# Rotary halves exchanged by on-chip transfers instead of a permutation product

## The reference

```python
def apply_rope(x, cos, sin):
    d2 = x.shape[-1] // 2
    x1, x2 = x[..., :d2], x[..., d2:]
    ...
    return jnp.concatenate([x1 * c - x2 * s, x1 * s + x2 * c], axis=-1)
```

## Time and profile before

| | |
|---|---|
| three runs | 1240.99, 1241.23 and 1244.12 us, median 1241.23 |
| the profiled execution | 1241.36 us, span 1239.5 us, 1.9 us around it |
| PE busy | 1217.6 us, 98% of the span |
| DVE, ACT, POOL busy | 848.9, 633.9 and 65.7 us |
| TensorE clock | 0.999 of full speed |

### The profile page before, as it was taken

How to read it: one execution, slowest core, us unless ns; L and a number is a source line. 1 busy time by engine, 2 the same in 40 slices (tenths; PEclk the granted TensorE clock), 3 DMA queues, 4 the chain that set the end, 5 groups by cost and what they waited for, 6 DMA issues and landing times. The chain is left out here.

```text
span 1239.5 us, 19652 instructions
## 1 busy us (share of the span) xinstructions
PE 1217.6 (98%) x7540; PEld 1064.9 (86%) x7540; DVE 848.9 (68%) x1241; ACT 633.9 (51%) x949; POOL 65.7 (5%) x58
## 2 busy tenths in 40 slices
PE   8999999999999999999999999999999999999997
PEld 6888889989998888888998888888899988888886
DVE  5776666667866766666799666666568976765564
ACT  6554456365536544445755555444475464544443
POOL 0000000300000000000430000000003200000000
PEclk9999999999999999999999999999999999999999
DMA  9575565565345665556555156555644724656550
GB/s 290 175 234 179 193 181 146 135 181 175 122 137 187 204 196 178 197 175 187 163 119 171 35 173 222 182 190 183 196 136 124 158 103 141 198 189 204 176 196 34
DMA packets 200914, 209.57 MB, mean 169 GB/s; under 512 B 58137, under 2 KB 177553, under 8 KB 200849
## 3 DMA queue, kind: packets, MB, share of 16 engines
q1 hardware_dynamic: 200400, 208.21, 54.2%
q10 hardware_dynamic: 448, 0.46, 0.1%
HBM read 207.61 MB, written 1.05 MB: 168 GB/s over the span
## 5 line engine op out<-in xcount | busy, mean ns | idle before, releaser
L1416 DVE TENSOR_TENSOR w_lo<-raw,w_hi 128x2048 fp32r<-128x2048 f32 (+2 forms) x192 | 433.0, 2257 | 174.0 <-ACT w_hi L1045 173.6
L2031 PE MATMUL bank<-n_both,w_hi 128*128 128x512 f32 x1216 | 432.8, 399 | 1.6 <-DVE w_lo L1416 1.6
L1045 ACT ACTIVATE w_hi<-raw 128x2048 fp32r<-128x2048 f32 (+2 forms) x192 | 360.7, 1880 | 97.9 <-PE bank L1970 76.2
L2032 PE MATMUL bank<-n_both,w_lo 128*128 128x256 f32 x1216 | 341.4, 281 | 0.0
L2031 PEld LDWEIGHTS bank<-n_both,w_hi 128*128 128x128 f32 x1216 | 228.5, 188 | 58.1 <-DVE w_lo L1416 1.5
L2032 PEld LDWEIGHTS bank<-n_both,w_lo 128*128 128x128 f32 x1216 | 229.7, 189 | 1.9
L1970 PE MATMUL bank<-n_both,w_hi 128*128 128x256 f32 (+3 forms) x960 | 175.9, 285 | 0.0
L1970 PE MATMUL bank<-w_hi,hid_hi 128*128 128x512 f32 x440 | 172.6, 392 | 0.2 <-DVE hid_lo L1497 0.2
L1970 PE MATMUL bank<-w_lo,hid_hi 128*128 128x512 f32 x440 | 171.7, 390 | 0.0
L1970 PE MATMUL bank<-w_hi,hid_lo 128*128 128x512 f32 x440 | 171.6, 390 | 0.0
L1063 ACT ACTIVATE scr<-bank 128x256 f32<-128x256 f32 x152 | 50.0, 381 | 207.5 <-PE bank L2032 207.5
(11 more groups left out here) (266 smaller groups left out, 1407.1 us busy)
## 6 DMA issues: line engine op xcount, KB each, us to landing
raw<-in_w_ff_dram SPq DMA_DIRECT2D x64, 1024.0 KB, 5.1
raw<-in_w_in_dram SPq DMA_DIRECT2D x31, 1024.0 KB, 5.3
raw<-in_ffn_down_dram SPq DMA_DIRECT2D x22, 1024.0 KB, 4.9
raw<-in_ffn_up_dram SPq DMA_DIRECT2D x21, 1024.0 KB, 5.3
raw<-in_ffn_gate_dram SPq DMA_DIRECT2D x20, 1024.0 KB, 5.3
raw<-in_w_out_dram SPq DMA_DIRECT2D x12, 1024.0 KB, 5.1
raw<-in_w_in_dram SPq DMA_DIRECT2D x12, 256.0 KB, 4.0
raw<-in_w_uq_dram SPq DMA_DIRECT2D x24, 128.0 KB, 3.9
```

Of the source, the lines that this page charges most:

```text
L1045: nc.scalar.activation(wh(s)[:, c0:n], raw[:, s % RING, c0:n], ACT.Copy).then_inc(hi_ready, 1)
L1416: V.tensor_tensor(wl(s)[:, c0:n], raw[:, s % RING, c0:n], wh(s)[:, c0:n].bitcast(f32), ALU.subtract).then_inc(lo_ready, 1)
L2031: MM(pb[:, :], w(s, 0)[:, c], n_both[:, k].rearrange("p a t -> p (a t)"), start=(k == 0), stop=False, skip_group_check=True)
L2032: return MM(pb[:, 0:T], w(s, 1)[:, c], xn(k, 0), start=False, stop=(k == KD - 1), skip_group_check=True)
```

## The change

PE's permutation product is gone, with its two matrices. In its place POOL issues transfers from SBUF to SBUF, one for each half, which bring the tile into a swap buffer with the halves exchanged: 4 transfers of 32 partitions where d2 is 32, and 8 of 16 partitions where it is 16. That is 28 in layer 0 and 48 in each of layers 1 and 2, 124 in all. POOL issues them in the rope step, ahead of its cosine product. The sign has moved into the sine tables. DVE waits for the landing, multiplies in place in the swap buffer, and adds as before. Layer 0 has two swap buffers and the others three, one of them `turn_s`.

Some steps stand elsewhere: sq1's rotation behind the first gate, ak's behind cq1's projection (and `toks` with it), kr's behind `uq` 0, uq's behind `ukv`; and DVE splits the second projection's slab behind the low halves, not ahead of them. The banks of the `wb` jobs are now given by number.

```diff
     rows = np.arange(P)
-    put("inv64", inv(32)[rows % 32][:, None])
+    put("inv64", sign(32) * inv(32)[rows % 32][:, None])
...
     put("cos_i", np.cos(angles(16, rows)))
-    put("sin_i", np.sin(angles(16, rows)))
+    put("sin_i", sign(16) * np.sin(angles(16, rows)))
 
     gamma = np.log1p(-np.exp2(-5.0 - np.arange(4)))
...
-    S += scores[0] + [("rope", 0, "nq1"), ("proj", 0, "sq1"), ("cmpt", "k")] + scores[1] + [("rope", 0, "sq1")] + turned[0]
-    S += gate[0] + [("cmp2", "k")] + scores[2] + weighted[0] + turned[1]
+    S += scores[0] + [("rope", 0, "nq1"), ("proj", 0, "sq1"), ("cmpt", "k")] + scores[1] + turned[0]
+    S += gate[0] + [("rope", 0, "sq1"), ("cmp2", "k")] + scores[2] + weighted[0] + turned[1]
...
-              ("stat", n), ("tables", l, "32"), ("tables", l, "64"), ("rope", l, "qi"), ("rope", l, "ak"),
-              ("toks", l), ("proj", l, "cq1"), ("rope", l, "ki"), ("proj", l, "cq2"), ("sums", l, 0),
+              ("stat", n), ("tables", l, "32"), ("tables", l, "64"), ("rope", l, "qi"),
+              ("proj", l, "cq1"), ("rope", l, "ak"), ("toks", l), ("rope", l, "ki"), ("proj", l, "cq2"), ("sums", l, 0),
...
-              ("rope", l, "rk"), ("proj", l, "rv"), ("rope", l, "rq"), ("rope", l, "kr"), ("rows", l),
-              ("uq", l, 0), ("ret", l, 0), ("ret", l, 1), ("ret", l, 2), ("ret", l, 3),
+              ("rope", l, "rk"), ("proj", l, "rv"), ("rope", l, "rq"), ("rows", l),
+              ("uq", l, 0), ("rope", l, "kr"), ("ret", l, 0), ("ret", l, 1), ("ret", l, 2), ("ret", l, 3),
               ("topk", l, 1, 0, 4), ("topk", l, 1, 4, 8), ("proj", l, "rg"), ("uq", l, 1),
-              ("retv", l), ("retn", l), ("rope", l, "uq"), ("uq", l, 2), ("s", l, "dsa", 0, 0),
-              ("s", l, "dsa", 0, 1), ("s", l, "dsa", 1, 0), ("s", l, "dsa", 1, 1), ("ukv", l),
+              ("retv", l), ("retn", l), ("uq", l, 2), ("s", l, "dsa", 0, 0),
...
+        swap = [swap0, wflat[:, 1536:2048], turn_s]
...
-                    job(("wb", 2 * n))
-                    job(("wb", 2 * n + 1), of_slab=True)
+                    job(("wb", 2 * n), 4 + 2 * n)
+                    job(("wb", 2 * n + 1), 5 + 2 * n, of_slab=True)
                 OT[st] = ohi[0]
...
+        SWAP, _landed, _user = {}, [0] * 3, [None] * 3
+        for u, r in RO.items():
+            b = r % 2 if u[0] == 0 else (r - RO[(u[0], "qi")]) % 3
+            _landed[b] += 16 * (8 if u[1] in ("qi", "ki", "kr", "uq") else 4)
+            SWAP[u] = (b, _landed[b], _user[b])
+            _user[b] = r
...
                     r = RO[st[1:]]
-                    src, n, nrow, _, (cos, _), dst = rotation(*st[1:])
+                    src, n, half, (cos, _), dst = rotation(*st[1:])
+                    b, _, user = SWAP[st[1:]]
+                    if user is not None:
+                        pool.wait_ge(rope_done, user + 1)
+                    if b == 2:
+                        pool.wait_ge(*((merged, 4) if st[1] == 1 else (oc_ready, NT + st[1] - 1)))
+                    pool.wait_ge(*free_count(XSC[st[1:]][0]))
+                    for c in range(0, P, half):
+                        other = c ^ half
+                        nc.gpsimd.dma_start(swap[b][c:c + half, 0:src.shape[1]], src[other:other + half]).then_inc(swap_in[b], 16)
                     pool.wait_ge(*free_count(XSC[st[1:]][0]))
                     pool.wait_ge(tab_ready, table_count(*st[1:]))
                     if r >= 2:
...
-                        ahead(SL[("proj", 0, "nq0") if n == 1 else ("proj", n // 2 - 1, "qi")], 1)
+                        first = SL[("proj", 0, "nq0") if n == 1 else ("proj", n // 2 - 1, "qi")]
+                        ahead(first, 0)
                         lower(n, (0, 1))
                         up_to_date(n, 3)
                         lower(n, range(2, 8))
+                        ahead(first, 1)
                     if n in (0, 2, 4, 5, 7):
                         take_mean(n).then_inc(mean_ready, 1)
...
                     r = RO[st[1:]]
-                    _, n, nrow, _, (_, sin), dst = rotation(*st[1:])
-                    pb = await_bank(dve, st)
+                    _, n, _, (_, sin), dst = rotation(*st[1:])
+                    b, landed, _ = SWAP[st[1:]]
+                    there = swap[b]
+                    dve.wait_ge(swap_in[b], landed)
                     dve.wait_ge(tab_ready, table_count(*st[1:]))
                     if st[2] == "kc":
-                        view = [x[:, 0:32].rearrange("p (g c) -> p g c", g=2)[:, :, 0:NCMP] for x in (turn_s, pb, turn_c[:, r % 2])]
+                        view = [x[:, 0:32].rearrange("p (g c) -> p g c", g=2)[:, :, 0:NCMP] for x in (there, turn_c[:, r % 2])]
                         s_ = sin[:, 31:T:16].unsqueeze(1).to_broadcast([P, 2, NCMP])
                     else:
-                        view = [x[0:nrow, 0:n * T].rearrange("p (a t) -> p a t", a=n) for x in (turn_s, pb, turn_c[:, r % 2])]
-                        s_ = sin.unsqueeze(1).to_broadcast([nrow, n, T])
-                    take_turn()
-                    V.tensor_tensor(view[0], view[1], s_, ALU.mult).then_inc(freed(st), 1)
-                    dve.wait_ge(*free_count(st))
+                        view = [x[:, 0:n * T].rearrange("p (a t) -> p a t", a=n) for x in (there, turn_c[:, r % 2])]
+                        s_ = sin.unsqueeze(1).to_broadcast([P, n, T])
+                    link(V.tensor_tensor(view[0], view[0], s_, ALU.mult))
                     dve.wait_ge(turnc_ready, r + 1)
                     if st[2] == "kc":
                         for g in range(2):
                             c = slice(64 * g, 64 * g + 64)
-                            last = V.tensor_tensor(kcR[c, g, 0:NCMP], view[2][c, g], view[0][c, g], ALU.add)
+                            last = V.tensor_tensor(kcR[c, g, 0:NCMP], view[1][c, g], view[0][c, g], ALU.add)
                         last.then_inc(rope_done, 1)
                     else:
-                        V.tensor_tensor(dst, view[2], view[0], ALU.add).then_inc(rope_done, 1)
-                    turn_used[0] = (rope_done, r + 1)
+                        V.tensor_tensor(dst, view[1], view[0], ALU.add).then_inc(rope_done, 1)
+                        if b == 2:
+                            turn_used[0] = (rope_done, r + 1)
                 elif kind == "xpe":
                     v = "kv".index(st[1])
                     if v == 0:
...
                         mm.then_inc(filled(("ukv", st[1], 2 + t)), 1)
-                elif kind == "rope":
-                    src, n, nrow, perm, _, _ = rotation(*st[1:])
-                    pe.wait_ge(*free_count(XSC[st[1:]][0]))
-                    pb = take(pe, st)
-                    if st[2] == "kc":
-                        mm = MM(pb[:, 0:32], perm, xs1[:, 0, 0:32], start=True, stop=True)
-                    else:
-                        mm = MM(pb[0:nrow, 0:n * T], perm, src, start=True, stop=True)
-                    mm.then_inc(filled(st), 1)
```

More of the change, by code:

```diff
@@ L50 @@
 NGAIN = _at
[L53 removed]
+CONST1 = [("ident", 128), ("inv64", 1), ("blk", 8), ("fold", 32),
           ("causal", 256), ("cmp_vis", 256), ("cos_a", 256), ("sin_a", 256), ("band", 256), ("cmp_mask", 256)]
@@ L77, in put, with sign @@
         where[:value.shape[0], at:at + n] = value
[L79 to L84, removed]
-            else:
-                m[c - half, c] = 1.0
-        return m
+    def sign(half):
+        return np.where((np.arange(P) // half) % 2 == 0, -1.0, 1.0).astype(np.float32)[:, None]
     put("ident", np.eye(P, dtype=np.float32))
-    put("perm64", perm(32))
-    put("perm32", perm(16))
     def inv(half):
@@ L111, in constants @@
     put("cos_a", np.cos(angles(32, rows)))
-    put("sin_a", np.sin(angles(32, rows)))
+    put("sin_a", sign(32) * np.sin(angles(32, rows)))
     put("cos_i", np.cos(angles(16, rows)))
-    put("sin_i", np.sin(angles(16, rows)))
+    put("sin_i", sign(16) * np.sin(angles(16, rows)))
     gamma = np.log1p(-np.exp2(-5.0 - np.arange(4)))
@@ L276, in two_blocks @@
         turn_c, turn_s = sb("turn_c", [P, 2, 512]), sb("turn_s", [P, 512])
+        swap0 = sb("swap0", [P, 512])
         probs, probsT = sb("probs", [P, 4, 512]), sb("probsT", [P, 2, 512])
@@ L384, in two_blocks @@
         turnc_ready, rope_done = sem("turnc_ready"), sem("rope_done")
+        swap_in = [sem(f"swap_in{i}") for i in range(3)]
         sink_seen, exp_done, pv_done, o_free = sem("sink_seen"), sem("exp_done"), sem("pv_done"), sem("o_free")
@@ L427, in job @@
         def job(key, b=None, freed_by=None, of_slab=False):
-            if b is None and idle[0] and key[0] in ("rope", "toks", "rank", "rows"):
+            if b is None and idle[0] and key[0] in ("toks", "rank", "rows"):
                 b = _small[0] % 4
@@ L729, in rotation @@
             buf = XSC[(l, "k" if name == "kk" else name)][1]
-            src = xs1 if buf == 2 else xs[:, buf, :].rearrange("p (a t) -> p a t", a=2)
-            c64, c32 = tab[l]["64"], tab[l].get("32")
```

(19 more changed lines are left out.)

7 lines of the change are left out of this document (3 added, 4 removed).

## The result

The changed kernel takes 1267.49 us (median of 4 runs, 1267.08 to 1267.97), the kernel before 1241.20 us beside it: a ratio of 1.0202, interval 1.0190 to 1.0215. It is slower by 26 us. The forecast was 1254 with a range of 1234 to 1276, so time and sign lie inside. That is partly luck: a price that was too high by 12 us stood in for part of some 25 us that the prediction had missed.

The account below looks back on a forecast made before the run. PE, busy 1217.6 of 1239.5 us, was taken as the bound. -5.0 (layer 0) - 1.8 (starts) + 7.6 + 10.6 (indexer) + 2 x 0.5 (retention) = +12.4 us, giving 1254 us, range 1234 to 1276.

Parts of the forecast that it names:

- The price of an issue: POOL's time to issue one transfer, called c: taken as 0.74 us, between 0.51 and 0.97.
- second rival: Issues cost what SP's do, c between 0.43 and 0.56: saving and wait cancel, 1238 to 1245 us; chance 0.12.
- signs of being wrong: Issue spacing below 0.43 us, landings far over 1.4 us, PE waits in layer 0, or PE's time after the scores shrinking.
- 606.6 + 20c: Layer 1's indexer: earliest start of scores after 20 issues by POOL; 621.4 at c = 0.74, 7.6 us later.
- 935.8 + 20c: Layer 2's indexer: earliest start of scores after 20 issues by POOL; 950.6 at c = 0.74, 10.6 us later.
- the term of 1.4 us: Landing time behind the last issue of a rotation's transfers, taken as 1.9 - 0.5 = 1.4 us.
- Both resume together, so nothing is caught up: Indexer, layers 1 and 2: PE and DVE resume together after the wait, so none of the 7.6 and 10.6 us is caught up.
- Retention: Layers 1 and 2, retention to dsa scores: DVE 0.9 to 2.8 us late, taken as +0.5 us a layer.
- counted POOL's products as delayed by DVE and not DVE by POOL's: At retention, rq's product on POOL would be late by up to 1.9 us under DVE's split.
- The 5.0 us stay: Layer 0: removing PE's rotation products saves 5.0 us, all kept, as landings come before or within 2 us of DVE.
- The starts: Mixers' starts: DVE's split moved behind the low halves removes PE waits of 0.35, 0.75 and 0.80 us, 1.8 us gained.
- The moved steps: Reordered rotations: sq1's needed late, cq1's move takes nothing from the wait; uq's pair moved behind the dsa scores.
- The ports: Rival: issues too are held while DVE runs two-operand SBUF products, 1263 us; chance 0.13 this or c above 1.0 exceeds 1270.

Follow-up runs that it names:

- Experiment 2: Changed kernel with qi's and ki's transfers issued ahead of the scaled tables in layers 1 and 2, ki's product ahead of cq1's and ak's: 1256.03 us, ratio 1.0121.
- experiment 3: Changed kernel with PE running products of zeros while it waits ahead of the indexer's scores and retention in layers 1 and 2: 1263.82 us, ratio 1.0181.
- experiment 6: Experiment 2's kernel with rq's and kr's rotations in layers 1 and 2 by PE's product, ki's transfers not behind ak's rotation: 1245.06 us, ratio 1.0021.
- experiment 11: Changed kernel with rq's and kr's cosine products in layers 1 and 2 done by DVE, not POOL: 1262.91 us, ratio 1.0175.
- experiment 10: Changed kernel with kr's 8 transfers in layers 1 and 2 issued some 30 us earlier, behind the second of the sums: 1263.51 us, ratio 1.0181.
- experiment 7: Transfers in layer 0 only, with its changed steps and the moved split; layers 1 and 2 with old list and PE's products: 1239.82 us, ratio 0.9986.
- experiment 9: Experiment 7's kernel with the compression's first input made behind sk's rotation, and qi by early transfers in layers 1 and 2: 1243.56 us, ratio 1.0009.
- experiment 12: Experiment 9's kernel without its early qi, and with nq1's rotation by PE's product too: 1237.10 us, ratio 0.9963.
- experiment 5: Kernel before with only DVE's split of the second projection's slab moved behind the low halves: 1239.76 us, ratio 0.9986.
- experiment 1: Changed kernel with its new order, but all 23 rotations again by PE's product: 1246.41 us, ratio 1.004.

## Why the prediction came out as it did

**The price of an issue** was mis-sized. Taken 0.74 us, measured 0.49. At SP's price the prediction's own sum gives 1242 us, so its second rival had the price right, and that rival's time misses by 25 us. What follows fills the gap: some 5 us on the chain ahead of the indexer's scores, 4.5 by the clock behind them, 12 up to the dsa scores and 5 in layer 0. The forecast's 1254 came near only because the price stood in for part of it. Two of its own signs of being wrong were there: landings far over 1.4 us, and a wait of PE in layer 0.

**The indexer.** Place, queue and form were right. The formula 606.6 + 20c gives 616.4 with c = 0.49, and it was 616.74, but with layer 1 beginning 2.0 us sooner: the chain was 2.3 us longer than reckoned. Some 0.8 of it arose ahead of the transfers (the tables were done only 1.2 us sooner). The rest was DVE's: qi's landing took 4.8 us for 1.4, and the split and ak's sum, 1.37 us beside POOL's product for 0.42, then stood ahead of ki. In layer 2, 935.8 + 20c = 945.6; 958.38 less the 9.9 us of late start is 948.5, 2.9 more. There it was ki's landing, 4.1 us for 1.4. So the term of 1.4 us failed in both layers, each time with a slab issued between the transfers. Experiment 2 shows that the issues' place makes the wait.

**"Both resume together, so nothing is caught up"** left out that PE resumes at a lower clock: 2.3 and 2.2 us behind the two waits, shown by experiment 3.

**Retention** was the largest miss: 0.5 us a layer forecast; the stretch up to the dsa scores grew by 5.5 and 5.4 us. The step that failed is the one that counted POOL's products as delayed by DVE and not DVE by POOL's: the five held operations make up 5.7 us in layer 1. The term of 1.4 us for a landing was wrong here too, but did not decide: the last of rq's transfers landed at 654.89 and the last of kr's at 659.80, and DVE came to them at 655.31 and 660.78. The sum had also left out DVE's product of kr behind the landing, 0.8 us. How the 6 us of experiment 6 would divide once the hold is gone isn't settled: with the hold removed for two rotations (experiment 11) 4.6 us came back in all, with kr's transfers issued early (experiment 10) 4.0.

**Layer 0.** "The 5.0 us stay" was wrong: nothing stayed. PE, sooner at the compression, waited 3.02 us ahead of its first product (245.51). I had asked whether a landing would be late, and not what PE would meet if it came sooner. PE's 95.00 of 95 us hid a chain just behind it: slab, ACT's copy, DVE's split, k's pair, the compression's input. Experiments 7, 9 and 12 show it.

**The starts** held in sum (1.8 forecast, 1.6 between medians in experiment 5, 1.9 in its profile). **The moved steps**, counted at nothing but for kr and uq, cost 5 us or more by experiment 1, of which part is unexplained.

**The ports.** The rival said an issue might be held under DVE's work. It isn't: the issues from 601.10 to 604.99, with a split of DVE from 601.66 to 603.95 beside them, kept to 0.49. By the Trainium skill (SBUF — State Buffer, Who interferes with whom) such a DVE operation holds only one of GpSimd's that reads SBUF; that descriptors pass it infers. The trace agrees. By the same section either side may block the other, by who comes first, and that half I had not used. The trace agrees in part: DVE's sum at 657.10 comes behind POOL's product of 656.47 and takes 1.64 us, but DVE's products at 655.31 and 660.78 come first by the profile and are long too, which the rule does not explain.

**Late landings.** In the changed kernel a transfer took 1.6 to 6.5 us from its issue to its landing, 3.0 in the median. The Trainium skill (Trainium Kernel Development and Optimization, Key Constraints) has it that transfers issued from SP, ACT and POOL run on the same 16 DMA engines and interleave; experiment 9's 6.1 us behind three slabs fit that, but no run took the slabs away.

## What to carry to other kernels

When work is taken off the engine that is always busy, look at what it reaches next: the saving lasts only to the first wait that was hidden just behind it, and each such chain has to be shortened too (experiments 7, 9 and 12). Trading a 0.86 us product for transfers puts 2 to 4 us of issues and 2 to 6 us of landing in front of its reader, so it pays only where reader and queues are far away. An in-order engine that waits early for a landing pays twice, with the idle time and with the work that then stands in front of the urgent piece.

## What the runs showed of the hardware

- A transfer within SBUF cost POOL 0.49 to 0.56 us to issue (once 0.68), whether of 16x512, 32x256 or 32x512, under DVE's splits too.
- A 128x512 product or sum of DVE beside or just ahead of a product of POOL took up to 2.35 us in place of 0.69 (1.63 and more around retention), and POOL's own up to 3.16 in place of 1.30 (experiment 10). Beside POOL's issues alone DVE's took 0.69.
- After waits of 3 to 10.5 us TensorE ran at 0.51 to 0.77 of full speed over the next 5 to 12 us. With the indexer's wait filled by products of zeros it did not slow down; behind retention, where the second wait stayed unfilled, it did.
